# The last expert but one ahead of the last: order of its down weights and of its down product in an MoE layer

## The chip, the cores and the metric

The kernel runs on one core of one Trainium2 chip. The metric is device time in microseconds (us) of one execution. Three executions of the kernel before took 1166.57, 1167.81 and 1168.5 us, so the median is 1167.81 us.

## What is computed

The reference is a trunk of two layers over 256 tokens of width 1024. Each layer has a mixing part (three kinds of attention between an input and an output projection) and then a mixture of experts. Every token goes to 2 of 32 experts, and an expert is three matrices:

```
def expert_block(args):
    xb, e = args
    h = jax.nn.silu(xb @ w_gate[e]) * (xb @ w_up[e])
    return h @ w_down[e]
```

The weighted results are summed per token and added to x. After the second layer there is one root-mean-square norm, and its result goes out. All expert weights are float32: gate and up of one expert are 4096 KB together, down is 2048 KB, so the 32 experts of one layer are 192 MB (of 1024 KB each) that have to come from memory.

## The kernel before, in words

**Tiles and rounds.** An expert takes up to 32 tokens (CAP). A layer runs four rounds (`ROUNDS`, variable `m`) of eight experts (`BODY`); tokens beyond 32 of an expert have a loop of their own, ahead of the last round. The change is in the last round, experts 24 to 31. In it `products(e)`, `turned(e)`, `down_of(e)` and `add(e)` are called with e from 0 to 7, so e = 7 is expert 31 (`LAST`) and e = 6 is expert 30, the last but one.

**One expert on the engines.** TensorE multiplies gate and up (`products`, `gate_up`, the matmul at L1746, 64 of them, in eight steps over the depth), ScalarE copies the result out of PSUM (`products_out`, recorded at L646), TensorE turns it and the gating weights (`turned`, L1757 and L1760), ScalarE takes the exponential (`exponent`, L811), VectorE forms silu(gate) * up in four operations (`hidden`, L1219 to L1222) and copies the turned gating weights (L1224). TensorE then multiplies by the down weights (`down_of`, `down`, L1770, 32 matmuls in four steps k), ScalarE copies the result (`y_out`, L646), and TensorE adds it, weighted, to the running sums of the tokens in PSUM (`add`, `scatter`, L1780, 16 matmuls). TensorE executes its instructions in the order in which they are written, and so does ScalarE.

**Places of weights.** Three places in SBUF hold a whole expert each (`place`), used in turn; expert 30 has place 2, which expert 27 had before it. Gate and up of the last expert have a fourth place, free since expert 3, and its down weights have four spare pieces of 512 KB (`spare`), free as early.

**Order of the loads.** All weights are loaded by one engine's instructions (SyncE, SP) through one queue, in the order written in `loads_of`, L146. For the last experts it is gate and up of 29, gate and up of 30, down of 29, gate and up of 31 (in two halves, `LAST_STEPS`, L570, each with a semaphore of its own), down of 30 (L577), down of 31 (in four pieces, L575). SP waits at L563 and L565 until a place is free: a load of gate and up waits for `gu_used`, a load of down weights for `d_used`, which `y_out` of the expert that had the place before increments (L838). What stands behind such a wait in SP's list waits with it.

**What follows.** In layer 0 SP goes on with the first input weights of layer 1 (L520); at L529 it waits for `y_out` of expert 31 before the small loads (L443) and the other input weights. TensorE goes on with four matmuls of zeros (L1443) and turns the new x (L1450). In layer 1 ScalarE and VectorE begin the final norm (L884, L1317) when the last `add` is done.

**keep_warm(n)** (L1713, matmul at L1716) adds n bfloat16 products of zeros, 512 columns each, to a running sum.

The end of the last round as it is written on TensorE before the change, with e = 7 for expert 31: after `add(5)` come ten of `keep_warm`, `products(7)`, `turned(7)`, `down_of(6)`, `add(6)`, `down_of(7)`, `add(7)`.

Of the kernel before, what the change touches and what calls it, by code (L numbers as in the profile page):

```python
# [52 lines left out]
BODY = 8  # L53
ROUNDS = N_EXPERTS // BODY
# [74 lines left out]
LAST = N_EXPERTS - 1  # L129
# [3 lines left out]
def place(e):  # L133

    return e if e < AHEAD else LATE if e == LAST else (e - AHEAD) % PLACES
# [10 lines left out]
def loads_of(m):  # L146

    first, last = max(m * BODY, AHEAD), (m + 1) * BODY
    if m == 0:
        order = [("d", AHEAD), ("gu", AHEAD + 1), ("d", AHEAD + 1)]  # L150
        return order + [("all", e) for e in range(AHEAD + 2, last)]
    if m < ROUNDS - 1:
        return [("all", e) for e in range(first, last)]
    order = [("gu", LAST - 2), ("gu", LAST - 1), ("d", LAST - 2), ("gu", LAST), ("d", LAST - 1), ("d", LAST)]
    return [("all", e) for e in range(first, LAST - 2)] + order


# [20 lines left out]
def at(layer, per_layer, n):  # L178

    return layer * per_layer + n  # L180
# [29 lines left out]
def trunk(nc, x_d, w_in_d, w_out_d, norm_mix, norm_ffn, bias_d, lam_q1, lam_k1, lam_q2, lam_k2,  # L210
# [3 lines left out]
    with ctx:  # L214
# [428 lines left out]
        def _(act):  # L643

            def copy(out, in_, **k):
                return nc.scalar.activation(out, in_, ACT.Copy, **k)  # L646
# [17 lines left out]
            for l in range(DEPTH):  # L664
# [145 lines left out]
                def neg_exp(b):  # L810
                    return nc.scalar.activation(e_neg, h_ps[:, :, 0:2, :].rearrange("p c h s -> p c (h s)"),  # L811
                                                ACT.Exp, scale=-1.0)

                for m in range(ROUNDS):
                    r = l * ROUNDS + m

                    def gathered(q):

                        for j in range(KD):
                            if j % 4 == 0:  # L820
                                act.wait_ge(wide_done, at(r, WIDE, gather_use(q) + j // 4))
                            copy(xg[:, j, :], wide_ps[:, j * P:(j + 1) * P], scale=gain_G[:, l, j:j + 1]).then_inc(wide_read, 1)

                    def products_out(e):

                        act.wait_ge(gu_done, at(r, BODY, e + 1))
                        act.sem_inc(gu_used[place(m * BODY + e)], 1)
                        copy(h_rows, gu_ps).then_inc(gu_read, 1)

                    def exponent(e):  # L830

                        act.wait_ge(h_done, at(r, BODY, e + 1))
                        neg_exp(e % 2).then_inc(neg_exped, 1)

                    def y_out(e):

                        act.wait_ge(wide_done, at(r, WIDE, y_use(e)))
                        act.sem_inc(d_used[place(m * BODY + e)], 1)  # L838
                        copy(y, tr[:, 0, 0:SEQ]).then_inc(wide_read, 1)

                    if m == ROUNDS - 1:
                        act.wait_ge(over_ready, l + 1)
                        act.sem_inc(passed["act"], 1)
                        done = act.value_load(over_n_i[0:1, 0:1], min_val=0, max_val=MOST_OVER * DEPTH)
                        more = act.value_load(over_n_i[0:1, 1:2], min_val=0, max_val=MOST_OVER)
                        with act.If(more > 0):
                            with act.Fori(0, more) as k:
                                i = done + k
                                act.wait_ge(o_wide, i * 2 + 1)
                                for j in range(KD):  # L850
                                    ins = copy(xg[:, j, 0:CAP], wide_ps[:, j * CAP:(j + 1) * CAP], scale=gain_G[:, l, j:j + 1])
                                ins.then_inc(o_wide_read, 1)
                                act.wait_ge(o_gu, i + 1)
                                copy(h_rows, gu_ps).then_inc(o_gu_read, 1)
                                act.wait_ge(o_h, i + 1)
                                neg_exp(0).then_inc(o_neg, 1)
                                act.wait_ge(o_wide, i * 2 + 2)
                                copy(y, tr[:, 0, 0:SEQ]).then_inc(o_wide_read, 1)
                    gathered(0)
                    products_out(0)  # L860
                    exponent(0)
                    for e in range(1, BODY - 1):
                        products_out(e)
                        y_out(e - 1)
                        exponent(e)
                        if e == QUAD - 1:
                            gathered(1)
                    if m < ROUNDS - 1:
                        y_out(BODY - 2)
                    products_out(BODY - 1)  # L870
                    exponent(BODY - 1)
                    if m == ROUNDS - 1:
                        y_out(BODY - 2)
                    y_out(BODY - 1)

                act.wait_ge(acc_done, at(l, 2 * TOK, 2 * TOK))
# [17 lines left out]
        def _(dve):  # L894
# [7 lines left out]
            for l in range(DEPTH):  # L902
# [174 lines left out]
                def finish_pair(s):  # L1077

                    kind, _, t = STEPS[s]
                    dve.wait_ge(pv_done, at(l, PV_USES, use_of(s) + 1))  # L1080
                    o = {"B": 0, "C": 2}[kind]
                    v.tensor_copy(mixT_up[:, t, o:o + 2, :].rearrange("p j s -> p (j s)"), pv[:, use_of(s) % 2, 0:2 * P]
                                  ).then_inc(pv_read, 1)
# [244 lines left out]
        def _(pe):  # L1328
# [6 lines left out]
            for l in range(DEPTH):  # L1335
# [377 lines left out]
                def keep_warm(n):  # L1713

                    for _ in range(n):
                        mm(sums[0], zeros[:, 0:P], zeros[:, P:P + 512], start=False, stop=False,  # L1716
                           skip_group_check=True)
# [68 lines left out]
                for m in range(ROUNDS):  # L1786
                    r = l * ROUNDS + m

                    def gu_landed(n):

                        if n == AHEAD:
                            pe.wait_ge(refill_in, 32 * (l + 1))
                        if n < LAST:
                            pe.wait_ge(gu_full[place(n)], gu_loads(l, n))
                        return gu_place[place(n)]
# [27 lines left out]
                    def products(e):  # L1823

                        q, i = e // QUAD, e % QUAD
                        gate_up(gu_landed(m * BODY + e), i * CAP,
                                at(r, READS, gather_read(q)) if i == 0 else None, m == 0 and e == 0,
                                m * BODY + e == N_EXPERTS - 1).then_inc(gu_done, 1)

                    def turned(e):  # L1830

                        q, i = e // QUAD, e % QUAD
                        pe.wait_ge(gu_read, at(r, BODY, e + 1))
                        if i == 0:
                            pe.wait_ge(pgate_ready, at(r, 2, q + 1))
                        if e > 0:
                            pe.wait_ge(pgt_read, at(r, BODY, e))
                        turns(i).then_inc(h_done, 1)

                    def down_of(e):  # L1840
                        rows_of = down_landed(m * BODY + e)
                        pe.wait_ge(hid_ready, at(r, BODY, e + 1))
                        pe.wait_ge(wide_read, at(r, READS, y_read(e) - 1))
                        down(rows_of, e % 2, m * BODY + e == N_EXPERTS - 1).then_inc(wide_done, 1)

                    def add(e):

                        pe.wait_ge(pgt_read, at(r, BODY, e + 1))
                        pe.wait_ge(wide_read, at(r, READS, y_read(e)))
                        if m == 0 and e == 0:  # L1850
                            pe.wait_ge(sums_open, l + 1)
                        scatter(e % 2, m == ROUNDS - 1 and e == BODY - 1)
# [28 lines left out]
                    for e in range(1, BODY - 1):  # L1881
# [3 lines left out]
                        add(e - 1)  # L1885
                        if e == QUAD - 1:
                            tokens(1)
                    if m == ROUNDS - 1:
                        keep_warm(10)
                    if m < ROUNDS - 1:  # L1890
                        down_of(BODY - 2)
                        products(BODY - 1)
                        turned(BODY - 1)
                    else:
                        products(BODY - 1)
                        turned(BODY - 1)
                        down_of(BODY - 2)
                    add(BODY - 2)
                    down_of(BODY - 1)
                    add(BODY - 1)  # L1900

# [22 lines left out]
def gather_use(q):  # L1924

    return 1 if q == 0 else 3 + QUAD - 1


def gather_read(q):

    return 1 if q == 0 else KD + QUAD


def y_read(e):

    return KD + 1 + e if e < QUAD - 1 else 2 * KD + 1 + e


def y_use(e):

    return 3 + e if e < QUAD - 1 else 5 + e
# [45 lines left out]
```

## Time and profile before

| what | value |
|---|---|
| executions | 1166.57, 1167.81, 1168.5 us; median 1167.81 us |
| the profiled execution's own time | 1168.1 us |
| its span, first to last instruction | 1166.2 us |
| mean granted TensorE clock | 0.911 of 2.4 GHz |
| bytes read from memory | 442.53 MB, 380 GB/s over the span |

The span is what the rows of the profile cover; 1.9 us of the execution lie outside it. Engines are PE (TensorE's matmuls), PEld (its weight loads), DVE (VectorE), ACT (ScalarE), POOL (GpSimd) and SP (SyncE); SPq and ACTq are the instruction streams of SP and ACT. All times in rows count from the first instruction. The granted clock is given as a share of full speed: 1.00 is 2.4 GHz, 0.50 is 1.2 GHz.

### The profile page before, as it was taken

Reading aid. Unit: us, or ns where it says so; the run is one execution under the profiler, and the core shown is the slowest. Engines: PE = TensorE matmul, PEld = TensorE weight load, DVE = VectorE, ACT = ScalarE, POOL = GpSimd, SP = SyncE. Lnnn points to the kernel's source line nnn. Section 1 sums busy time; section 2 is a strip of 40 time slices with the busy share of each in tenths; the row PEclk is TensorE's granted clock in tenths of the full one; section 3 lists DMA queues with packets and bytes.
Section 4 is the critical chain, followed back from the end, with each engine's and each line's share of the span. In section 5 each row is a group of like instructions: output and inputs, shape, how many; then the busy total and the mean of one; then the engine's idle time right before and its main releaser. Section 6 shows DMA issues by size and latency. Waiting matters only on the chain.

```text
span 1166.2 us, 23346 instructions
## 1 busy us (share of the span) xinstructions
PE 920.8 (79%) x10299; PEld 578.4 (50%) x10299; DVE 329.8 (28%) x972; ACT 212.6 (18%) x623; POOL 16.3 (1%) x38
## 2 busy tenths in 40 slices
PE   9999999666766676768799999987575758676775
PEld 5876666333433343435378766654343424334442
DVE  3656552211120112112137465521111111111112
ACT  2234332010101010101112442310110011101012
POOL 1000000000000000000010000000000000000000
PEclk9999999987888889889999999999788987887898
DMA  7966499999999999999995466999999999999996
GB/s 307 407 240 257 193 383 439 416 431 430 436 431 433 430 429 423 430 425 419 422 384 223 162 237 253 383 432 430 432 428 436 429 429 423 425 429 431 425 423 269
DMA packets 27544, 445.13 MB, mean 382 GB/s; under 512 B 8880, under 2 KB 10288, under 8 KB 13744
## 3 DMA queue, kind: packets, MB, share of 16 engines
q1 hardware_dynamic: 26880, 443.49, 90.3%
q8 instruction: 84, 1.38, 0.5%
q10 hardware_dynamic: 560, 0.10, 0.0%
q14 instruction: 20, 0.16, 0.0%
HBM read 442.53 MB, written 1.05 MB: 380 GB/s over the span
## 4 chain that ended last, share of the span: by engine, by line
DMA 49%; PE 47%; issue 1%; DVE 1%; ACT 1%; POOL 0%; ACTq 0%; POOLq 0%; SPq 0%; DVEq 0%
DMA ring_xb<-in_experts 49%; PE pv L1746 13%; PE pj L1371 8%; PE tr L1770 6%; PE pj L1377 2%; PE pj L1481 2%; PE pj L1601 2%; PE pj L1780 2%; PE pj L1576 1%; PE pj L1610 1%; PE lg L1401 1%; PE pv L1760 1%; PE tr L1411 1%; PE tr L1677 1%; PE tr L1730 1%
## 5 line engine op out<-in xcount | busy, mean ns | idle before, releaser
L1746 PE MATMUL pv<-ring_xb,xT 128*32 128x256 f32 x3840 | 286.2, 459 | 181.7 <-DMA ring_xb<-in_experts 181.7
L1746 PEld LDWEIGHTS pv<-ring_xb,xT 128*32 128x32 f32 x3840 | 135.7, 127 | 320.7 <-DMA ring_xb<-in_experts 197.5
L1219 DVE TENSOR_SCALAR arena<-arena 128x128 f32<-128x128 f32 x64 | 14.5, 227 | 660.2 <-ACT arena L811 659.9
L1770 PE MATMUL tr<-ring_xb,arena 128*32 128x256 f32 x1920 | 116.7, 383 | 19.8 <-issue 15.2
L646 ACT ACTIVATE arena<-pv 128x256 f32<-128x256 f32 x64 | 24.6, 385 | 499.6 <-PE pv L1746 499.6
L1371 PE MATMUL pj<-xT,ring_xb 128*128 128x256 f32 x448 | 100.2, 381 | 0.0
L1770 PEld LDWEIGHTS tr<-ring_xb,arena 128*32 128x32 f32 x1920 | 64.2, 110 | 63.7 <-issue 21.6
L1371 PEld LDWEIGHTS pj<-xT,ring_xb 128*128 128x128 f32 x448 | 84.1, 190 | 13.1 <-issue 1.1
L1780 PE MATMUL pj<-arena 32*128 32x256 f32 x512 | 72.5, 399 | 6.8 <-ACT arena L646 6.8
L1780 PE MATMUL lg<-arena 32*128 32x256 f32 x512 | 72.5, 400 | 0.0
L646 ACT ACTIVATE arena<-tr 128x256 f32<-128x256 f32 (+3 forms) x106 | 41.3, 408 | 152.3 <-PE tr L1770 130.2
L1730 PE MATMUL tr<-arena,rows 128*128 128x128 f32 x448 | 58.9, 294 | 10.6 <-issue 10.6
L1730 PEld LDWEIGHTS tr<-arena,rows 128*128 128x128 f32 x448 | 56.0, 207 | 15.4 <-issue 15.4
L1220 DVE RECIPROCAL arena<-arena 128x128 f32<-128x128 f32 x64 | 61.0, 953 | 2.2
L1780 PEld LDWEIGHTS pj<-arena 32*128 32x128 f32 x512 | 44.4, 184 | 23.5 <-issue 22.3
L646 ACT ACTIVATE xT<-tr,gains 128x128 f32<-128x128 f32 x128 | 36.4, 370 | 66.8 <-PE tr L1730 66.7
L1780 PEld LDWEIGHTS lg<-arena 32*128 32x128 f32 x512 | 43.7, 184 | 0.0
L1760 PE MATMUL pv<-con,arena 128*32 128x128 f32 x1024 | 41.2, 279 | 0.0
L1757 PE MATMUL pv<-con,arena 128*128 128x128 f32 x128 | 32.3, 334 | 9.4 <-ACT arena L646 9.4
L1757 PEld LDWEIGHTS pv<-con,arena 128*128 128x128 f32 x128 | 20.2, 206 | 37.2 <-issue 19.8
L646 ACT ACTIVATE arena<-pj 64x256 f32<-64x256 f32 (+2 forms) x48 | 21.0, 442 | 71.0 <-PE pj L1371 52.4
L699 ACT ACTIVATE arena<-arena,nmax 128x128 f32<-128x128 f32 (+1 forms) x64 | 28.6, 447 | 25.2 <-DVE nmax L1046 24.8
(235 smaller groups left out, 793.7 us busy)
## 6 DMA issues: line engine op xcount, KB each, us to landing
ring_xb<-in_experts SPq DMA_DIRECT2D x48, 6144.0 KB, 22.4
ring_xb<-in_experts SPq DMA_DIRECT2D x18, 2048.0 KB, 11.0
ring_xb<-in_experts SPq DMA_DIRECT2D x6, 4096.0 KB, 28.7
ring_xb<-in_w_in_chunks SPq DMA_DIRECT2D x10, 2048.0 KB, 22.0
ring_xb<-in_experts SPq DMA_DIRECT2D x12, 1024.0 KB, 7.8
ring_xb<-in_w_out_halves SPq DMA_DIRECT2D x4, 2048.0 KB, 30.6
arena<-in_experts SPq DMA_DIRECT2D x2, 4096.0 KB, 12.7
arena<-in_experts SPq DMA_DIRECT2D x4, 2048.0 KB, 38.6
```

The costliest lines, as they stand in the source:

```text
L646: return nc.scalar.activation(out, in_, ACT.Copy, **k)
L699: ins = nc.scalar.activation(prob[:, s % 2, m * nk(t):(m + 1) * nk(t)], logit[:, s % 2, m * nk(t):(m + 1) * nk(t)], ACT.Exp, bias=nmax[:, ...
L1220: own.link(v.reciprocal(e_neg, e_neg))
L1371: ins = mm(out, w[:, j], xT[:, j, :], start=(j == 0), stop=(j == KD - 1))
L1377: ins = mm(out, src[:, j, t * P:(t + 1) * P], weights(i, n)[:, j, c:c + m], start=(j == 0), stop=(j == KD - 1))
L1481: ins = mm(bank[:, 0:R5], xT_raw[:, j, t * P:(t + 1) * P], weights(0, n5)[:, j, :], start=(j == 0), stop=(j == KD - 1))
L1730: ins = mm(wide_ps[:, j * n:(j + 1) * n], rows[:, t, j * P:(j + 1) * P], pick[:, t, 0:n], start=(t == 0), stop=(t == TOK - 1))
L1746: ins = mm(gu_ps[i * CAP:(i + 1) * CAP, :], xg[:, j, c:c + CAP], w, start=(j == 0), stop=(j == KD - 1), tile_position=(0, i * CAP), skip_g ...
L1757: turn_(h_ps[:, c].rearrange("p h s -> p (h s)"), by_step[:, c], ident)
L1760: ins = mm(pgt_ps[k * CAP:(k + 1) * CAP, t * P:(t + 1) * P], pgate[:, t, i, :], ident, start=True, stop=True, tile_position=(0, k * CAP), ...
L1770: ins = mm(tr[i * CAP:(i + 1) * CAP, 0, 0:SEQ], hid[:, b, k % 2, k // 2, :], rows_of[k][:, SEQ * i:SEQ * (i + 1)], start=(k == 0), stop=(k ...
L1780: ins = mm(sums[i][:, SEQ * t:SEQ * (t + 1)], pgT[r, b, t, :], y[r, :], start=False, stop=last, tile_position=(i * CAP, 0), skip_group_che ...
```

## The change

In the load order the down weights of expert 30 go ahead of gate and up of expert 31. TensorE does the down product and the sum of expert 30 ahead of gate and up of expert 31, with six products of zeros behind each instead of ten in one place. ScalarE's order follows.

```
-    order = [("gu", LAST - 2), ("gu", LAST - 1), ("d", LAST - 2), ("gu", LAST), ("d", LAST - 1), ("d", LAST)]
+    order = [("gu", LAST - 2), ("gu", LAST - 1), ("d", LAST - 2), ("d", LAST - 1), ("gu", LAST), ("d", LAST)]
...
(ScalarE)
-                    if m < ROUNDS - 1:
-                        y_out(BODY - 2)
+                    y_out(BODY - 2)
                     products_out(BODY - 1)
                     exponent(BODY - 1)
-                    if m == ROUNDS - 1:
-                        y_out(BODY - 2)
                     y_out(BODY - 1)
...
(TensorE)
-                    if m == ROUNDS - 1:
-                        keep_warm(10)
                     if m < ROUNDS - 1:
                         down_of(BODY - 2)
                         products(BODY - 1)
                         turned(BODY - 1)
+                        add(BODY - 2)
                     else:
+                        down_of(BODY - 2)
+                        keep_warm(6)
+                        add(BODY - 2)
+                        keep_warm(6)
                         products(BODY - 1)
                         turned(BODY - 1)
-                        down_of(BODY - 2)
-                    add(BODY - 2)
                     down_of(BODY - 1)
                     add(BODY - 1)
```

Rounds 0 to 2 issue the same instructions in the same order as before.

## Rows read from the trace of the kernel before

**Rows 1.** Page: busy time per engine; shares of the chain that ended last.
```profile
PE 920.8 (79%) x10299; PEld 578.4 (50%) x10299; DVE 329.8 (28%) x972; ACT 212.6 (18%) x623; POOL 16.3 (1%) x38
...
DMA 49%; PE 47%; issue 1%; DVE 1%; ACT 1%; POOL 0%; ACTq 0%; POOLq 0%; SPq 0%; DVEq 0%
```

**Rows 2.** Chain of waits, end of layer 1: start us, us, what.
```profile
1117.05 33.16 DMA ring_xb<-in_experts
...
1150.25 1.98 PE tr L1770 x32
...
1154.01 1.96 PE tr L1770 x32
...
1157.86 0.70 ACT arena L884 x2
```

**Rows 3.** Chain of waits, end of layer 0, and its next transfer of weights.
```profile
538.02 34.69 DMA ring_xb<-in_experts
572.75 3.65 PE tr L1770 x32
...
578.18 1.91 PE tr L1770 x32
...
581.87 0.97 PE tr L1443 x4
...
780.96 19.91 DMA ring_xb<-in_experts
```

**Rows 4.** Loads by line: issue durations, first and last start us; time to landing. Layer 1.
```profile
L570 SPq DMA_DIRECT2D arena<-in_experts x2: 438/440/443, 1104.7 to 1105.2; - x2
...
DMA to landing us min/median/max: 35.7/37.9/40.1
```

**Rows 5.** The same for the pieces of down of 31: layer 1, then layer 0.
```profile
L575 SPq DMA_DIRECT2D arena<-in_experts x2: 447/1556/2664, 1117.9 to 1118.9; - x2
...
DMA to landing us min/median/max: 34.1/35.2/36.4
...
L575 SPq DMA_DIRECT2D arena<-in_experts x2: 432/3702/6971, 538.9 to 539.8; - x2
...
DMA to landing us min/median/max: 35.6/36.8/38.0
```

**Rows 6.** Timeline, layer 1: start us, us, engine line operation [idle before, releaser].
```profile
1130.66 3.83 PE L1746 MATMUL pv<-ring_xb,xT 128*32 128x256 f32 x64 [2.06 <-DMA ring_xb<-in_experts]
...
1139.50 2.33 PE L1716 MATMUL pj<-zeros 128*128 128x512 bf16 x10
...
1141.77 2.03 PE L1746 MATMUL pv<-arena,xT 128*32 128x256 f32 x32
...
1145.35 2.03 PE L1746 MATMUL pv<-arena,xT 128*32 128x256 f32 x32 [1.55 <-DMA arena<-in_experts]
...
1148.40 0.64 PE L1760 MATMUL pv<-con,arena 128*32 128x128 f32 x16
...
1151.00 0.29 DVE L1222 TENSOR_TENSOR arena<-pv,arena 128x128 f32<-128x128 f32 x1
```

**Rows 7.** Timeline, layer 0.
```profile
542.56 5.16 PE L1746 MATMUL pv<-ring_xb,xT 128*32 128x256 f32 x64 [2.57 <-DMA ring_xb<-in_experts]
...
567.80 2.02 PE L1746 MATMUL pv<-arena,xT 128*32 128x256 f32 x32 [2.05 <-DMA arena<-in_experts]
...
573.44 0.29 DVE L1222 TENSOR_TENSOR arena<-pv,arena 128x128 f32<-128x128 f32 x1
```

**Rows 8.** Stretches, layer 0: length, busy time of each engine, granted clock, DMA share, GB/s.
```profile
571.00:572.00 1.00, 0.49 (x16) 0.22 (x9) 0.13 (x1) 0.28 (x1) 0.00 (x0) 1.00 0.98 393
572.00:573.00 1.00, 0.25 (x4) 0.20 (x8) 0.96 (x2) 0.00 (x0) 0.00 (x0) 0.87 1.11 452
573.00:574.00 1.00, 1.00 (x12) 0.40 (x8) 0.93 (x4) 0.00 (x0) 0.00 (x0) 0.50 1.03 424
...
576.00:577.00 1.00, 0.34 (x4) 0.00 (x0) 0.00 (x0) 0.38 (x1) 0.00 (x0) 0.92 1.01 426
```

## The prediction

> **What bounds the kernel now.** I read the page first, for the shares. TensorE is busy for 79% of the span, but the chain that ended last gives 49% to transfers and 47% to TensorE [rows 1], so the bound changes from stage to stage and has to be read at the place of the change, twice, once per layer. Then I read the chain of waits there. At the end of layer 1 the load of the down weights of expert 30 is issued at 1117.05 and lands 33.16 us later, at 1150.21; TensorE starts the down product of 30 at 1150.25, the down product of 31 follows at 1154.01, and the final norm begins at 1157.86 [rows 2]. At the end of layer 0 the same load lands at 572.7, the down product of 30 starts at 572.75, that of 31 at 578.18, and the first work of layer 1 at 581.87 [rows 3]. So 7.6 us pass in layer 1, and 9.1 in layer 0, from this landing to the end of the layer, and all of it is TensorE with two copies between.
>
> Is the queue or TensorE last there? The loads by line tell the landings. In layer 1 the halves of gate and up of 31 land at 1104.7 + 35.7 = 1140.4 and 1105.2 + 40.1 = 1145.3 [rows 4], the down weights of 30 at 1150.2, and the last piece of the down weights of 31 at 1118.9 + 36.4 = 1155.3; in layer 0 that piece lands at 539.8 + 38.0 = 577.8 [rows 5]. A transfer of 2048 KB thus has a slot of 4.9 us. The down product of 31 takes 1.96 us in four steps, so in layer 1 its last step starts at about 1155.4, right at the landing of the last piece: **layer 1 already ends as early as its bytes allow**, but for the 2.5 us of last step, copy and sum. In layer 0 the last step starts 1.8 us after the landing, for a reason that comes below.
>
> **The change, part by part.**
>
> *Load order.* The bytes and their number of issues stay. The down weights of 30 take the slot in which the first half of gate and up of 31 lands now (1140.4), and the halves move to 1145.3 and 1150.2 in layer 1. In layer 0 the row of the second half starts at 567.80, behind its landing [rows 7], and the next slot ends at 572.7; the second half now lands there. The last piece keeps 1155.3 and 577.8.
>
> *The wait on SP.* The load of 30's down weights waits for the copy of expert 27's result, so gate and up of 31 and its down weights now stand behind this wait; before, gate and up of 31 were issued at 1104.7. The wait ends at 1117.05 in layer 1 and 538.02 in layer 0. From there to the landing are 33.16 and 34.69 us; the new landing is 9.8 us earlier and its own slot is 4.9 us, so about 18.5 us of other transfers are still queued when the wait ends. That backlog hides it: cost 0. Were it gone, each us without queued work would cost one.
>
> *Down product, copy and sum of 30.* They leave the path behind the landing and lie now in the stretch where TensorE waits for gate and up of 31. In layer 1: down product from 1140.4, 2.0 us; six products of zeros at 2.33 / 10 each [rows 6], 1.4; sum, 1.2 (copy and sum fill the 1.8 us from 1152.2 to 1154.01 in rows 2, and the copy is hidden here); six more, 1.4: ready at 1146.4. The first half (landed 1145.3) is multiplied until 1148.5, and TensorE then waits for the second, at 1150.2. Two more zero products than before cost 0.5 us, hidden by that wait of 1.8 us (2.3 in layer 0). The copies on ScalarE are hidden by the zero products.
>
> *Gate and up, turning, exponential and silu of 31.* These are now what stands behind the landing at 1150.2. Their length is in the rows: the second half starts at 1145.35 and the multiplication that completes the hidden values ends at 1151.29, so 5.94 us [rows 6]; in layer 0 from 567.80 to 573.73, 5.93 us [rows 7]. Before, both lay beside the transfer of 30's down weights. After it, they lie beside the down weights of 31, whose last piece comes only 5.1 us after the second half; so they cover the transfer and stick out.
>
> With 0.1 us from VectorE to TensorE, the down product of 31 starts in layer 1 at 1150.25 + 5.94 + 0.1 = 1156.3 instead of 1154.01: **+2.3 us**. Behind it nothing changes (3.85 us to the norm). In layer 0: 572.75 + 5.93 + 0.1 = 578.8 instead of 578.18: **+0.6 us**. What is behind the end of layer 0 shifts whole: from 572.7 to 781 the chain of waits holds no transfer [rows 3], and the first weights of layer 1 queue behind those of 31 as before.
>
> *Why layer 0 shows less.* There the down product of 30 took 3.65 us against 1.98 in layer 1 [rows 2, 3]: the granted clock was 0.50, that is 1.2 GHz, from about 572.75 to 576.1, and 1.00 (2.4 GHz) around it [rows 8]. It cost the kernel before 1.7 us on its path, so in layer 0 a slowed end is compared with a new one at full clock. Without that stretch both layers would pay 2.3.
>
> *The clock after the change.* The low stretch came when TensorE had been idle for 2.05 us, then 0.6 and 1.2, with 3.1 us of work between [rows 7, 8]. After the change it waits 2.3 us (layer 0; 1.8 in layer 1) between the halves of gate and up, then 0.6 for the copy, and after 1.1 us of turning (it ends at 1149.0 where the hidden values are ready at 1151.3, rows 6) 2.3 us for ScalarE and VectorE, a wait beside which it now has no other work. Everything after either wait is on the path. Other waits of that length went both ways: the 64 matmuls behind 2.06 us of idle time took 3.83 us [rows 6], those behind 2.57 took 5.16 [rows 7]. The price in a layer is bounded by 0 and, for one such stretch, by 1.7 us (3.4 us at half speed, rows 8), with a second one possible; I take 1.1 us per layer, since one stretch is likely in each, and the copy and the VectorE work inside it don't slow down. For both: **+2.2 us**, with ends 0 and 3.4.
>
> The rows show a fall of the clock at 572.75 with no idle time on TensorE above 2.05 us just before it [rows 7, 8]. The Trainium skill ("TensorE: Matmul & The Clock Gate", section "Why this matters for your kernels") warns only of idle gaps longer than any that stands on this path before or after the change. By that rule the clock stays at 2.4 GHz and the sum lacks this last term; the trace of layer 0 disagrees with it.
>
> **The sum.** Own time of the profiled execution 1168.1 us (span 1166.2 and 1.9 around it). Plus 0.6 and 2.3 is 1171.0; plus 2.2 is 1173.2. The median of the runs shown is 0.3 below the profiled one, so the forecast is **1172.9 us**, 5.1 us or 0.44% slower.
>
> **The rivals.**
>
> *The clock holds.* Nothing falls to 1.2 GHz at the end of either layer: 1171.0 - 0.3 = 1170.7 us. For it: in layer 1 before, three waits of 1.55, 0.6 and 1.2 us went by at 1.00. Against it: the last wait of 2.3 us has only 1.1 us of work ahead of it.
>
> *Only the last layer pays.* Some slack between the layers (a transfer awaited in layer 1) takes up layer 0's part: 1168.1 + 2.3 - 0.3 = 1170.1 us. Against it: the chain through layer 1's mixing part is TensorE alone.
>
> *Not slower: the new chain is covered.* If the work from the second half of gate and up to the hidden values fits beside the down weights of 31, then the down product, copy and sum of 30 are simply gone from the end. Layer 1 gains nothing, since its last step starts at its landing already; layer 0 gets back its 1.7 us: 1168.1 - 1.7 - 0.3 = 1166.1 us. It decides at a chain of 3.6 us, which would have the down product of 31 start by 1153.9; both layers show 5.9. For a gain that could be measured a second source would be needed, such as luck with the clock elsewhere.
>
> *The queue runs dry.* The wait for the copy of 27 starves the queue: the landings of 31 move later, by what the wait lasts beyond the backlog, say 5 us in a layer: 1175 to 1180 us. Against it the backlog of 18.5 us.
>
> **How the numbers follow.** Chances: forecast 0.60 (its own range 1171.6 to 1174.6), clock holds 0.22, only the last layer 0.06, covered 0.07, queue dry 0.05. About 0.2% (2.3 us, so 1165.5 to 1170.1) is what a measurement of this kernel can tell from no change. Slower by more holds the forecast, most of the second case (0.18), half of the third (0.03) and the last: 0.86. Faster by more: 0.03, of the covered case. Within: 0.11. The range goes down to 1169.6, to hold the second and third case, and up to 1175.0: sum without clock 1170.7, two full low stretches (3.4), and 0.9 for part of a third.
>
> **What would show it.** In the profile after: the down product of 30 starts at the landing of 30's down weights, near 1140 in layer 1 (plus layer 0's shift), with 2 us or less of wait before the first half of gate and up; the second half of it starts at its landing, and the chain of waits goes from that transfer through L1746, the copy, L1757, L1760, the exponential and VectorE's four operations to the down product of 31, some 6.0 us later, which no longer waits for any transfer. The clock row shows 0.50 for some us between the second half and the end of each layer. SP's issues of gate and up of 31 stand right behind the one at 538 and 1117 and the transfers show no gap. I am wrong if VectorE is done with 31 within 4 us of that landing, if the end of layer 0 shifts and the end of the mixing part does not, or if the landings of 31's last piece move.

## The result, and the profile after

The changed kernel takes 1175.7 us (median of 4 executions, 1174.86 to 1176.79) against 1168.15 us (4 executions, 1166.57 to 1170.29): slower by a ratio of 1.0068, 95% interval 1.0053 to 1.0082. The profiled execution took 1174.86 us with a span of 1173.0 us, 6.8 us more than before in both. The direction and the mechanism are as forecast; the forecast of 1172.9 us and the upper end of its range, 1175.0, are too low.

Lines moved by the edit: L1743 is the gate and up matmul (L1746 before), L1767 the down matmul (L1770), L1777 the sum (L1780), L1440 the zeros at the start of layer 1 (L1443), L1216 to L1219 the hidden values, L881 the start of the norm (L884).

The shares of the page hardly move, as a change at two places should have it:

```profile
PE 921.8 (79%) x10303; PEld 578.2 (49%) x10303; DVE 329.8 (28%) x972; ACT 212.2 (18%) x623; POOL 16.3 (1%) x38
...
DMA 49%; PE 47%; issue 2%; DVE 1%; ACT 1%; SPq 0%; POOL 0%; ACTq 0%; POOLq 0%; DVEq 0%
```

The chain of waits of the kernel after (start us, us, what), end of layer 0, which answers to [rows 3]:

```profile
539.42 33.78 DMA arena<-in_experts
...
573.25 2.06 PE pv L1743 x32
...
575.42 0.39 ACT arena L646
...
575.85 0.51 PE pv L1754 x2
576.36 0.62 PE pv L1757 x16
...
577.57 0.96 DVE arena L1217
...
578.89 0.30 DVE arena L1219
...
579.23 3.64 PE tr L1767 x32
...
584.66 0.97 PE tr L1440 x4
...
783.76 20.13 DMA ring_xb<-in_experts
```

and end of layer 1, which answers to [rows 2]:

```profile
1121.07 32.24 DMA arena<-in_experts
...
1153.35 2.06 PE pv L1743 x29
...
1159.34 3.49 PE tr L1767 x32
...
1164.72 0.70 ACT arena L881 x2
```

The transfer ahead of the end is now the second half of gate and up of 31 (into `arena`), no longer the down weights of 30. Behind it stands everything that makes the hidden values of 31, 5.98 us long, and then a down product of 3.64 and 3.49 us where the one of 31 took 1.91 and 1.96 before. The stretches say why (length, busy time of PE, PEld, DVE, ACT, POOL, granted clock, DMA share, GB/s); this is layer 0:

```profile
577.00:578.00 1.00, 0.00 (x0) 0.00 (x0) 0.65 (x2) 0.28 (x1) 0.00 (x0) 1.00 0.94 398
578.00:579.00 1.00, 0.00 (x0) 0.00 (x0) 0.93 (x3) 0.00 (x0) 0.00 (x0) 1.00 1.11 471
579.00:580.00 1.00, 0.77 (x8) 0.39 (x12) 0.51 (x2) 0.00 (x0) 0.00 (x0) 0.66 1.07 432
580.00:581.00 1.00, 1.00 (x16) 0.52 (x12) 0.00 (x0) 0.00 (x0) 0.00 (x0) 0.50 0.88 375
```

TensorE is idle while VectorE works, and its clock falls as it gets the hidden values: the mean is 0.66 over the stretch in which the down product starts, then 0.50, that is 1.2 GHz. In the timeline of layer 1 the wait has its name:

```profile
1153.35 2.02 PE L1743 MATMUL pv<-arena,xT 128*32 128x256 f32 x32 [1.62 <-DMA arena<-in_experts]
...
1159.34 0.90 PE L1767 MATMUL tr<-xT,arena 128*32 128x256 f32 x8 [2.30 <-DVE arena L1219]
```

### The profile page after: what moved, and what is told of

Same layout as the page of the kernel before. It is cut to its first block, busy times and chain, and to the rows that moved or that the text cites. A ratio compares the mean times of both kernels' runs of the same rounds, so it can differ in the third digit from the quotient of the medians.

```text
span 1173.0 us, 23354 instructions
## 1 busy us (share of the span) xinstructions
PE 921.8 (79%) x10303; PEld 578.2 (49%) x10303; DVE 329.8 (28%) x972; ACT 212.2 (18%) x623; POOL 16.3 (1%) x38
## 4 chain that ended last, share of the span: by engine, by line
DMA 49%; PE 47%; issue 2%; DVE 1%; ACT 1%; SPq 0%; POOL 0%; ACTq 0%; POOLq 0%; DVEq 0%
DMA ring_xb<-in_experts 43%; PE pv L1743 13%; PE pj L1368 8%; DMA arena<-in_experts 6%; PE tr L1767 6%; PE pj L1374 2%; PE pj L1478 2%; PE pj L1598 2%; PE pj L1777 1%; PE pj L1573 1%; PE pj L1607 1%; PE lg L1398 1%; PE pv L1757 1%; PE tr L1408 1%; PE pv L1754 1%
## 5 line engine op out<-in xcount | busy, mean ns | idle before, releaser
L1743 PE MATMUL pv<-ring_xb,xT 128*32 128x256 f32 x3840 | 285.4, 458 | 184.3 <-DMA ring_xb<-in_experts 184.3
L1743 PEld LDWEIGHTS pv<-ring_xb,xT 128*32 128x32 f32 x3840 | 135.3, 127 | 322.9 <-DMA ring_xb<-in_experts 200.3
L1216 DVE TENSOR_SCALAR arena<-arena 128x128 f32<-128x128 f32 x64 | 14.5, 227 | 670.8 <-ACT arena L811 670.5
L1767 PE MATMUL tr<-ring_xb,arena 128*32 128x256 f32 x1920 | 115.0, 379 | 19.8 <-issue 15.2
L1767 PEld LDWEIGHTS tr<-ring_xb,arena 128*32 128x32 f32 x1920 | 64.2, 109 | 62.8 <-issue 20.3
L1777 PE MATMUL pj<-arena 32*128 32x256 f32 x512 | 72.5, 400 | 5.3 <-ACT arena L646 5.3
L1777 PE MATMUL lg<-arena 32*128 32x256 f32 x512 | 72.5, 400 | 0.0
L1777 PEld LDWEIGHTS pj<-arena 32*128 32x128 f32 x512 | 44.3, 184 | 22.5 <-issue 21.3
L1777 PEld LDWEIGHTS lg<-arena 32*128 32x128 f32 x512 | 43.7, 184 | 0.0
```

The costliest lines, as they stand in the source:

```text
L1743: ins = mm(gu_ps[i * CAP:(i + 1) * CAP, :], xg[:, j, c:c + CAP], w, start=(j == 0), stop=(j == KD - 1), tile_position=(0, i * CAP), skip_g ...
L1767: ins = mm(tr[i * CAP:(i + 1) * CAP, 0, 0:SEQ], hid[:, b, k % 2, k // 2, :], rows_of[k][:, SEQ * i:SEQ * (i + 1)], start=(k == 0), stop=(k ...
L1777: ins = mm(sums[i][:, SEQ * t:SEQ * (t + 1)], pgT[r, b, t, :], y[r, :], start=False, stop=last, tile_position=(i * CAP, 0), skip_group_che ...
```

## The experiments

All are timed beside the kernel before, in three groups, on one chip each; its medians there were 1168.21, 1168.32 and 1168.48 us. A ratio is to it, with its 95% interval.

**The changed kernel again.** 

> The changed kernel once more, beside its variants. Two theories of the 7.5 us it lost against 5.1 forecast. Clock theory: the chain behind the second half of gate and up (3 us in both layers together) and the down product of expert 31 at 1.2 GHz in both layers (3.2 us in the profile), more in other executions where a low stretch also meets the matmuls between the halves. Queue theory: the new load order makes the landings themselves later, and the clock adds only what the kernel before had too. Both expect 1174.5 to 1177 us here, some 7.5 us above the kernel before.

1175.28 us (1175.07 to 1177.85), ratio 1.0066 (1.0053 to 1.0079). Its profile has, at the end of layer 0, a low stretch twice as long: it begins in the down product, as before, and goes on over the sum and the start of layer 1:

```profile
572.67 2.06 PE pv L1743 x32
...
578.65 3.14 PE tr L1767 x32
...
582.43 0.80 PE pj L1777 x2
...
584.52 1.75 PE tr L1440 x4
```

From the landing to the next layer's first work 11.85 us pass, in the changed kernel's profile 11.41.

**Zero products in the wait for the hidden values.** Edit:

```
                     down_of(30), keep_warm(6), add(30), keep_warm(6), products(31), turned(31)
+                    keep_warm(9)
                     down_of(31), add(31)
```

> The changed kernel with nine products of zeros between turned(31) and down_of(31), in the wait of 2.3 us for ScalarE and VectorE. Clock theory: the down product of 31 takes 1.95 us instead of 3.5 in both layers, so 3.2 us less than the changed kernel: 1172.5 us. Queue theory: at most 0.5 us less, 1175 us or more.

1171.91 us (1170.54 to 1172.83), ratio 1.0028 (1.0017 to 1.0039): 3.4 us below the changed kernel of the same group. Nothing else was touched, and the added products by themselves could only take time, so this part of the loss is the clock. The down product is at full speed in both layers (1.98 us), but in this execution the low stretch of layer 0 met the second half of gate and up instead:

```profile
572.56 3.17 PE pv L1743 x32
...
579.72 1.98 PE tr L1767 x32
...
1152.82 2.06 PE pv L1743 x32
...
1158.80 1.98 PE tr L1767 x32
```

**Zero products in both waits.** `warm_silu` and six more in `gate_up`, ahead of the wait for the second half:

```
                             if in_pieces and j == first:
+                                if n > 0:
+                                    keep_warm(6)
                                 pe.wait_ge(last_steps_in[n], 16 * (l + 1))
```

> As warm_silu, and six products of zeros more between the two halves of gate and up of 31, in the wait of 1.6 to 2.4 us for the second half. Clock theory: what is left of low clock on the path goes too, 0 to 1 us below warm_silu: 1171.3 to 1172.5 us, that is 3 to 4 us above the kernel before, and the chain from the second half to the down product of 31 still 5.9 us long. Queue theory: like the changed kernel, 1175 us.

1171.82 us (1171.33 to 1173.37), ratio 1.0035 (1.0022 to 1.0048). No difference from `warm_silu` can be told in the medians. Its profile is the change at full clock (layer 0):

```profile
573.28 2.06 PE pv L1745 x32
...
579.26 1.98 PE tr L1769 x32
...
583.02 0.97 PE tr L1440 x4
```

9.74 us from the landing to the next layer, where the forecast without its clock term had 6.0 + 3.7 = 9.7.

**Only layer 1, and only layer 0.** The load order, ScalarE's order and TensorE's order depend on `l == 1` (or `l == 0`); the other layer runs as before.

> The change made in layer 1 alone; layer 0 has loads, products and copies in the order of before. If each layer pays for itself and layer 0's share shifts all that follows: layer 1's share in the profile was 4.0 us (2.3 of chain, 1.6 of clock), so about 4 us above the kernel before and 3 to 3.5 below the changed kernel: 1172.2 us. Rival: slack between the layers hides layer 0's share, so this is as slow as the changed kernel, 1175 us or more.

> The change in layer 0 alone. layer1_only lost 3.7 us; if the layers pay separately and layer 0's share shifts what follows, this loses the rest of the changed kernel's 7.1 to 7.5: 3.4 to 3.8 us, 1171.7 us. Rival: layer 0's share is partly hidden by the transfers of layer 1, less than 2 us lost, 1170 us or below.

Layer 1 alone: 1171.88 us (1169.32 to 1175.98), ratio 1.0031 (1.0018 to 1.0045). Layer 0 alone: 1171.78 us (1168.49 to 1172.72), ratio 1.0023 (1.0015 to 1.0032). Against the medians of their groups that is 3.7 and 3.3 us, 7.0 together, and the changed kernel in the first group lost 7.1. Each layer pays for itself; nothing between the layers takes up layer 0's part.

The profiled execution of layer 0 alone is the quickest of its twelve (1168.49 us), and its layer 0 shows what the others do not: behind the same wait of 2.30 us the down product of 31 runs at full clock (L1774 here, in the chain and in the timeline).

```profile
578.19 1.98 PE tr L1774 x32
...
578.19 0.64 PE L1774 MATMUL tr<-xT,arena 128*32 128x256 f32 x8 [2.30 <-DVE arena L1226]
```

**Gate and up of 31 in four pieces.** `warm_silu` with

```
-LAST_STEPS = ((0, 4), (4, 8))
+LAST_STEPS = ((0, 4), (4, 6), (6, 7), (7, 8))
```

> warm_silu, with gate and up of expert 31 loaded in four pieces (steps 0 to 3, 4 and 5, 6, 7) instead of two halves, so that 8 matmuls (0.5 us) instead of 32 (2.0 us) stand behind the last landing. If the chain behind that landing is what the changed kernel pays with (2.3 us per layer at full clock), 1.5 us per layer go: 3 us below warm_silu, 1168.9 us. Rival: the end is set by transfers or by the sums, and pieces change nothing, 1171.9 us; or more issues in the queue cost, slower than that.

1169.03 us (1167.66 to 1170.61), ratio 1.0005 (0.9996 to 1.0014): 2.9 us below `warm_silu` (other group), 3 expected. Only 8 matmuls stand behind the last landing:

```profile
572.84 0.70 PE pv L1743 x8
...
577.46 1.98 PE tr L1767 x32
...
581.38 0.81 PE tr L1440 x3
```

The down product starts 4.6 us behind the landing instead of 6.0. So the length of the chain behind this landing is what the change pays with at full clock, and it can be bought down. Within this group `pieces_warm` is 1.9 us above the kernel before with zero products (`before_warm`, below), where the chains differ by 2 x (4.62 - 3.76) = 1.7.

**The same pieces in the kernel before.** 

> The kernel before with gate and up of 31 in the same four pieces. There the chain of gate and up lies beside the load of the down weights of 30: by the chain theory nothing changes, 1168.2 us within 0.6. If pieces help by something else (less waiting, a warmer clock), 1 to 3 us less here too.

1172.51 us (1169.42 to 1174.71), ratio 1.0034 (1.0022 to 1.0046). This missed: 4.2 us slower, where "nothing" was expected and only a gain was named as the other way. The timeline of its layer 1:

```profile
1146.11 0.66 PE L1746 MATMUL pv<-arena,xT 128*32 128x256 f32 x8 [0.30 <-DMA arena<-in_experts]
...
1147.79 0.64 PE L1760 MATMUL pv<-con,arena 128*32 128x128 f32 x16
1151.00 3.64 PE L1770 MATMUL tr<-ring_xb,arena 128*32 128x256 f32 x32 [2.57 <-DMA ring_xb<-in_experts]
```

and its stretches:

```profile
1150.00:1151.00 1.00, 0.00 (x1) 0.00 (x1) 0.93 (x4) 0.00 (x0) 0.00 (x0) 0.50 0.98 393
...
1157.00:1158.00 1.00, 1.00 (x12) 0.40 (x12) 0.00 (x0) 0.00 (x0) 0.00 (x0) 0.50 0.00 0
```

The pieces let TensorE finish gate and up of 31 earlier, and so it waits 2.57 us for the down weights of 30, where it waited 1.21 before:

```profile
1150.25 1.93 PE L1770 MATMUL tr<-ring_xb,arena 128*32 128x256 f32 x32 [1.21 <-DMA ring_xb<-in_experts]
```

The clock falls within the longer wait (0.72 over the stretch from 1149) and is at 0.50 in all stretches from 1150 to 1159, over the first down product, the sum and most of the second down product. Layer 0 of this profile is as before, with its own low stretch on the down product of 30 (3.66 us).

**And with ten zero products ahead of `down_of(30)`.** 

> before_pieces with ten products of zeros ahead of down_of(30). The pieces end the gate and up of 31 about 1.5 us earlier, so that TensorE waits 2.7 us instead of 1.2 for the down weights of 30; if the 4.2 us that before_pieces lost are a low clock behind this longer wait, the zero products give all of it back: 1167 to 1168.2 us. Rival: more and smaller issues cost in the queue, then it stays at 1171 to 1172.5 us.

1167.98 us (1166.59 to 1169.81), ratio 0.9995 (0.9985 to 1.0005). All of the 4.2 us come back, with the same number of transfers: they were the clock, not the queue. Some of what the zero products give may be what they give the kernel before, 0.8 to 1.2 us (below).

**The new loads with the old order of work.** The edit is the line in `loads_of` alone.

> The new order of loads with the old order of work: down product, copy and sum of 30 behind turned(31), so they fill the wait for the hidden values. At full clock the down product of 31 starts 1.4 us later per layer than in the changed kernel (copy and sum of 30 stick out of the wait of 2.3 us), but this wait now has work that holds the clock. Theory: 1.4 per layer above warm_silu, 1174.7 us, within 1 us of the changed kernel. Rival: the moved work was worth its whole 3.7 us per layer, then 1179 us; or it was worth nothing, 1171.9 us.

1175.87 us (1173.85 to 1177.64), ratio 1.0061 (1.0046 to 1.0075). Layer 0:

```profile
573.15 3.69 PE pv L1746 x32
...
578.46 1.77 PE tr L1770 x32
...
582.02 1.91 PE tr L1770 x32
...
585.86 0.81 PE tr L1443 x3
```

The down product of 30 does fill the wait for the hidden values, and the clock is up there. But it no longer fills the time before gate and up of 31: TensorE waits 4.00 us for the first half, the clock falls inside that wait, and both halves run low (3.64 and 3.69 us, for 2.03 at full speed):

```profile
567.00:568.00 1.00, 0.00 (x0) 0.00 (x0) 0.00 (x0) 0.00 (x0) 0.00 (x0) 0.50 0.92 389
...
568.20 3.64 PE L1746 MATMUL pv<-arena,xT 128*32 128x256 f32 x32 [4.00 <-DMA arena<-in_experts]
```

From the landing of the second half to the down product of 31 pass 8.87 us, less 1.66 of clock 7.2. With the work moved it is 5.98, and in the kernel before at full clock 3.76: the new place of the loads costs 3.4 us per layer, and the moved work gives 1.2 of it back. In the medians the kernel cannot be told from the changed one. The clock does not explain that: in this profile it costs 1.7 and 1.3 us behind the landings, in the changed kernel's 1.7 and 1.5. By the chains it should be some 2 us slower, as its profiled execution is (1176.96 us, against 1174.86 and 1175.29), so for its median (6 executions, 1173.85 to 1177.64) the account stays open.

**Zero products in the waits of the kernel before.** Six between the halves of gate and up, as in `warm_both`, and four ahead of `down_of(30)`:

```
                         turned(BODY - 1)
+                        keep_warm(4)
                         down_of(BODY - 2)
```

> The kernel before with six products of zeros between the halves of gate and up of 31 and four ahead of down_of(30). Clock theory: the low stretch on the down product of 30, 1.7 us in layer 0 of the profile, goes, and the median falls by 0.5 to 1.7 us (it is not in every execution): 1166.5 to 1167.7 us. Rival: the zero products delay the work behind them or the low stretch has another cause, 1168.2 us or more.

> The kernel before with zero products in both waits, once more, beside the others: 1167.1 us, 0.5 to 1.2 below the kernel before.

1167.14 us (1166.11 to 1168.21), ratio 0.999 (0.9981 to 0.9998); again 1167.73 us (1166.54 to 1170.21), ratio 0.9991 (0.9982 to 1.0001). Its chain, end of layer 0:

```profile
573.13 1.98 PE tr L1772 x32
...
576.89 1.99 PE tr L1772 x32
...
580.82 0.81 PE tr L1443 x3
```

(L1772 is the down matmul here.) Both down products are at full clock. Its median is below the kernel before both times, by about 0.1%, with an interval clear of 1 only the first time: the edge of what these runs tell.

## Why the prediction was wrong, by its own steps

**The order of loads and landings: right.** The second half of gate and up takes the slot of the down weights of 30 (573.25, was 572.7). The last piece of the down weights of 31 lands in layer 0 before the down product that needs it begins:

```profile
L575 SPq DMA_DIRECT2D arena<-in_experts x2: 435/3268/6100, 540.4 to 541.3; - x2
...
DMA to landing us min/median/max: 34.6/35.8/37.0
```

that is 541.3 + 37.0 = 578.3, the product starts at 579.23. This landing moved by 0.5 us, which I had named as a sign of being wrong; it is the 0.5 us of that execution (below). The queue did not run dry: the issues of gate and up of 31 stand behind the wait, at 538.9 and 539.4, and land 28.7 and 33.8 us later; the core moves 421 to 423 GB/s from 540 to 570, against 417 to 424 before.

**The chain behind the landing: right, in both layers.** Forecast +0.6 and +2.3. Measured from landing to down product of 31: 5.98 in layer 0 against 578.18 - 572.75 = 5.43 [rows 3], so +0.55; 5.99 in layer 1 against 3.76 [rows 2], +2.23. `pieces_warm` shows it by a second way, and the two kernels with one changed layer show that the layers add up.

**The clock term: the right mechanism, mis-sized; this is the step that failed.** I wrote "I take 1.1 us per layer" with a bound of 1.7 for one stretch, 2.2 us in all, on the ground that part of a stretch would fall on the copy and the VectorE work. In the profile the down product of 31 and what follows it cost 1.73 us more in layer 0 (3.64 against 1.91) and 1.53 in layer 1 (from the product to the norm 5.38 against 3.85): 3.3 us instead of 2.2. Timed, the zero products give 3.4 us back. The stretch did not spread over the copy and VectorE: in this profile it began at the start of the down product and fell nearly whole on it. It can also be longer than the one stretch that I counted per layer, as the repeated profile shows. The wait for the down weights of 30 in `before_pieces` (2.57 us) is the same case.

What decides whether the clock falls behind such a wait stays open. The wait of 2.30 us stands right ahead of the down product at six ends of a layer that have a profile and no zero products there; five times the product ran low, once, in `layer0_only`, at full clock. The changed kernel's wait of 2.35 us ahead of the second half in layer 0 went by at full clock, and in `warm_silu` one of 2.04 at the same place did not.

The Trainium skill ("TensorE: Matmul & The Clock Gate", "Why this matters for your kernels") warns of idle gaps longer than any in this place of the changed kernel; its runs disagree, since the clock fell in both layers with no single wait above 2.35 us. Only `loads_only` has a wait as long as the row means (4.00 us), and there the clock fell too.

**What was not in the sum.** Landings 0.5 us later in layer 0 and 0.3 more in layer 1. The first is there before the changed order begins: the whole load of expert 28, first line before, second after, already lands 0.55 us later:

```profile
511.06 21.19 DMA ring_xb<-in_experts
```

```profile
511.20 21.60 DMA ring_xb<-in_experts
```

All profiles together say the same. The transfer of this slot in layer 0 lands at 572.2 to 573.2 in the seven with the new order there and at 572.5 to 573.3 in the six with the old one. From the start of layer 1's turning of x to its landing in layer 1 it is 567.4 to 568.3 us in the seven with the new order and 567.1 to 568.3 in five with the old (in `layer0_only`, the sixth, nothing waits for it). So the 0.8 us belong to the execution, not to the change.

The four terms 0.55 + 2.23 + 3.26 + 0.81 add up to 6.85 us, and the norm starts 6.86 us later. The medians lie 7.55 apart, because the profiled execution after was the quickest of its four, by 0.8; a longer low stretch like that in the repeated profile would do that, but the other executions have no trace, so it stays open.

The forecast was 2.8 us too low. The clock term is 1.1 of it and the only term of the sum that was clearly mis-sized, but with 3.3 in its place the sum would give 1174.0, still inside the range. The rest is 0.8 of landings and 1.1 of the step from the profiled execution to the median: I took it as 0.3 down, and it was 0.8 up. These two were scatter between executions, for which the sum had no term.

**The rivals.** "The clock holds" (1170.7) fell with the profile and with `warm_silu` (1171.9), which comes near it only because zero products hold the clock. "Only the last layer pays" fell with the two single-layer kernels. "Covered" would need a chain of 3.6 us and got 6.0. "The queue runs dry" (1175 to 1180) came nearest in time, but that is chance: no transfer was late by the new order.

At full clock on both sides the change costs 4.4 to 4.8 us: `warm_both` is 3.6 above the kernel before of its group, `before_warm` and its repetition 1.2 and 0.75 below theirs. The chain gives 2 x 2.2 = 4.4 (5.98 against 3.76 us). This also says what the +0.6 of layer 0 rests on: one profile, in which the kernel before lost 1.7 us to the clock. In the medians it loses about 1 us, so timed the change without its clock costs 3.6 us, not 2.9. The intervals, over 1 us to either side, are too wide to settle this.

## What to carry to other kernels

Ask of the last transfers which one has the longest work behind its landing, and let that one come first: here moving 2048 KB of down weights, with 3.8 us of product, copy and sum between their landing and the last down product, ahead of gate and up, with 6.0 us, cost 2.2 us per layer at full clock, and 3.4 with the old order of work. A wait on the critical path can cost twice if TensorE has nothing else to do in it: in this kernel the product behind it ran at 1.2 GHz five times of six, so price it so, not at a mean, or fill the wait. And an engine that finishes earlier ahead of a transfer that does not has a longer wait and can make the kernel slower, as the four pieces did in the kernel before.

## What the runs showed that was not expected

Loading gate and up of expert 31 in four pieces instead of two halves made the kernel before 4.2 us slower through the clock alone, with TensorE at 0.50 for some 10 us. The low stretch began in the wait and went on through a down product, a sum and most of a second down product, with a wait of 0.7 us between them. Ten products of zeros, 2.3 us of work that nothing reads, removed all of it.
